# Eight slots for the first key pages of a paged attention step, and key pages fetched in four pieces of 32 keys

## The chip, the core and the metric

The kernel runs on one core of a Trainium2 chip. A core has five engines with a queue of instructions each: TensorE (PE in the profile; its weight loads stand as PEld), VectorE (DVE), ScalarE (ACT), GpSimd (POOL) and SyncE (SP). They wait for each other through semaphores. Data is moved between HBM and the on-chip memory (128 partitions) by 16 DMA engines; almost all of this kernel's transfers are issued from SP, in SP's program order. The metric is the time of one execution on the device, in microseconds (us).

## What is computed

One inference step of a decoder of two layers, in float32: a retention layer, then shared keys and values (K/V), then a block-sparse attention layer (MoBA). There are 256 prompt tokens and 8 sequences of 8 new tokens, the "sample", each with 256 past tokens. The past keys and values lie in a paged pool in HBM, and a table says which page belongs where:

```python
PAST_LEN, PAGE_SIZE, DEC_BATCH, DEC_SEQ = 256, 128, 8, 8
MOBA_HEADS, MOBA_HD = 8, 128
# cache_k, cache_v: (n_phys, PAGE_SIZE, MOBA_HEADS, MOBA_HD)    page_table: (8, 2)

def moba_sample(q, k_new, v_new, cache_k, cache_v, page_table, rel_bias):
    def per_seq(args):
        q_s, kn, vn, pages = args
        k_past = cache_k[pages].reshape(past, MOBA_HEADS, MOBA_HD)
        v_past = cache_v[pages].reshape(past, MOBA_HEADS, MOBA_HD)
        ...
        return moba_attend(q_s, q_pos, k_s, v_s, rel_bias)
```

So there are 16 key pages and 16 value pages, each of 128 tokens x 8 heads x 128 numbers, 512 KB. Every query scores all 256 past keys of its sequence and the new ones before it, per head; then softmax with a bias by distance, the sum over the values, a gate, and an output projection.

## The kernel before

All matrix products of the layers are done on one core. A projection's weights are cut into **chunks** of 1 MB: the list `chunks` holds them, and `make_schedule` writes one list of `steps` by hand. Each engine runs through the same list and does its own part of each step. So a step's place in the list is its place in every engine's queue. A chunk's weights land in one of three buffers of `w_raw` (`load_chunk`, issued two chunks ahead on SP, at the step `CHUNK`); ACT rounds them to `w_hi` (L1229) and DVE takes the rest, `w_lo` (L1569), a quarter at a time (steps `WS`); PE multiplies three terms of the two (L927, L930, L911). The chunks that matter here follow one another: four of the query projection (`mq`, up to about 330 us), four of the keys (`mk`, each 3 tiles in two halves), then four of the values (`mv`). The chunks `mk` and `mv` come from `w_kv`.

Among these the 16 **key pages** of the past are read and scored. A page n goes through these steps:

- On SP, `load_page` (L709): it waits until the slot is free, reads the page's number from `pages` into a register (L717), and issues the transfer. A key page is fetched in four pieces (L724). Piece g holds two heads of all 128 keys and goes to partitions 32g to 32g+31, four runs of 1 KB in each. A value page is one transfer to 128 partitions (L719). SP does these at the steps `ME` and `KP`.
- On DVE, the step `KP` n: a 32x32 block transpose of the page (L1860). It waits for `cache_loaded` of the slot and raises `kt_done`.
- On PE, the steps `KS` 0 to 3, each after four pages: 128 small matmuls (L1101) of the queries with the transposed keys.

Before the change there are six **slots** for key pages: four in `cache` and two in the tensor `mkT` (`early_pages`), which is free until the new keys are written to it. Page n takes slot n mod 6 for the first twelve pages, and one of the four in `cache` from then on. The first six pages are asked for without a wait, at `ME` 1 to 6. From page 6 on a page's load waits on `kt_done`: page 6 for the transpose of page 0, page 7 for that of page 1, and so on. SP's queue is in order, so whatever stands behind such a wait is issued after it, the weight chunks too. ACT waits with `KX`, its first write to `mkT`, until twelve pages are transposed (L1498), since the last pages that lie in `mkT` are 10 and 11.

The new value rows of the sample, `mvs`, and the new key rows, `rows`, are written later. POOL clears the unused half of `mvs` and of `rows` at the step `MB`, ahead of the queries' spread.

Of the kernel before, what the change touches and what calls it, by code (L numbers as in the profile page):

```python
# [33 lines left out]
P = 128  # L34
D = 1024
KT = D // P
TP, TS = 256, 64
# [3 lines left out]
MH, HD = 8, 128  # L41
# [7 lines left out]
NST = 8  # L49
NCP, NSLOT = 4, 6  # L50
FAR = PAST + NEW - 1
# [64 lines left out]


def page_slot(n):

    return n % NSLOT if n < 2 * NSLOT else (n - 2 * NSLOT) % NCP  # L120

# [190 lines left out]
def build(nc, a):  # L312
# [3 lines left out]
    with ctx:  # L316
# [3 lines left out]
        def sem(name):  # L320
            return ctx.enter_context(nc.semaphore(name))
# [90 lines left out]
        cache = mb("cache", [P, NCP, D])  # L412
# [3 lines left out]
        mvs = mb("mvs", [P, D])  # L416
        rows = mb("rows", [P, 3, 512])
# [75 lines left out]
        line_stored, lines_stored = sem("line_stored"), sem("lines_stored")  # L493
        bias_loaded, tb_loaded, bn_done = sem("bias_loaded"), sem("tb_loaded"), sem("bn_done")
        wide_cleared, pads_cleared = sem("wide_cleared"), sem("pads_cleared")
        wide_filled, wide_reset, kt_done, own_q_done = sem("wide_filled"), sem("wide_reset"), sem("kt_done"), sem("own_q_done")
# [67 lines left out]
        def page_at(n):  # L564

            at = page_slot(n)
            return cache[:, at, :] if at < NCP else early_pages[:, at - NCP, :]

# [98 lines left out]
        def _(sp):  # L667
# [41 lines left out]
            def load_page(n):  # L709

                m, vals = (n - 16, True) if n >= 16 else (key_page(n), False)
                before = n - (NCP if n >= 2 * NSLOT + NCP else NSLOT)
                if before >= 16:
# [4 lines left out]
                if vals:  # L718
                    sp.dma_start(page_at(n), a["cache_v"][bass.ds(page, 1)].rearrange("o p h d -> p (o h d)"))\  # L719
                        .then_inc(cache_loaded[page_slot(n)], 16)  # L720
                    return
                src = a["cache_k"][bass.ds(page, 1)].rearrange("o (c i) h d -> i (o c) (h d)", i=32)
                for g in range(4):
                    sp.dma_start(page_at(n)[32 * g:32 * g + 32, :].rearrange("p (c x) -> p c x", c=4), src[:, :, 256 * g:256 * g + 256])\  # L724
                        .then_inc(cache_loaded[page_slot(n)], 16)
# [19 lines left out]
            for step in steps:  # L745
# [65 lines left out]
                elif kind == "US":  # L811
                    store_pair(4 * step[1] + 3)
                    load_pair(4 * step[1] + 6)
                elif kind == "ME" and 1 <= step[1] <= NSLOT:
                    if step[1] == 1:
                        sp.wait_ge(pages_loaded, 16)
                        await_ret_over(sp)
                        sp.dma_start(knw[:, :], bass.AP(a["k_norm_w"].tensor, 0, [[0, P], [1, HD]])).then_inc(knw_loaded, 16)
                    load_page(step[1] - 1)
                elif kind == "KP":  # L820
                    n = step[1]
                    if 1 <= n <= 16 - NSLOT:
                        load_page(n + NSLOT - 1)
                    elif n >= 16 - NCP + 1:
                        load_page(n + NCP - 1)
                elif kind == "SE" and step[1] == 1:
# [30 lines left out]
        def _(pe):  # L857
# [83 lines left out]
            for step in steps:  # L941
# [221 lines left out]
                elif kind == "PN":  # L1163
                    pe.wait_ge(pads_cleared, 1)
                    await_read(pe, sb_bank(3), "SB", 3)
# [45 lines left out]
        def _(act):  # L1211
# [27 lines left out]
            for step in steps:  # L1239
# [257 lines left out]
                elif kind == "KX":  # L1497
                    act.wait_ge(kt_done, 2 * NSLOT)  # L1498
                    for i in range(2):
# [448 lines left out]
        def _(pool):  # L1948
# [28 lines left out]
            for step in steps:  # L1977
# [42 lines left out]
                elif kind == "MB":  # L2020
# [5 lines left out]
                    pool.wait_ge(wide_cleared, 1)  # L2026
                    pool.memset(mvs[TS:P, :], 0.0)
                    pool.memset(rows[TS:P, 2, :], 0.0)
# [5 lines left out]
                elif kind == "KS" and step[1] == 3:  # L2034
                    await_ks(pool, 3)
                    pool.wait_ge(bn_done, 1)
                    for n, g in enumerate((1, 3)):
                        if n:
                            pool.wait_ge(wide_reset, 1)
                        pool.memset(slots[32 * g:32 * g + 32, :, :, 16:16 + NEW], 0.0).then_inc(wide_reset, 1)  # L2040
# [53 lines left out]
```

## Time and profile before

| | us |
|---|---|
| median of 3 runs | 506.27 |
| lowest and highest of them | 503.84, 506.54 |
| the profiled execution, whole | 503.63 |
| its span in the trace | 501.6 |

| engine | busy us | share of the span |
|---|---|---|
| PE | 490.5 | 98% |
| PEld | 423.9 | 85% |
| DVE | 357.9 | 71% |
| ACT | 261.2 | 52% |
| POOL | 97.5 | 19% |

The profiled execution took 503.63 us, of which the trace's span holds 501.6; the 2.0 us between them lie around it. Times in the trace count from the span's start. PE is busy nearly all the time, so a wait matters where it stops PE; the profile's table of waits says which instruction was late and what ended its wait. The views of the DMA engines give three things for a stretch: the mean busy share of the 16 engines (a share over 1 means that packets overlap on an engine), the rate in GB/s, and how many packets were under 2 KB.

### The profile page before, as it was taken

The page shows a single profiled execution, that of the slowest core. Times are in us where ns is not written, and L with a number is a line of the kernel's source. Part 1 is how long each engine was busy: PE and PEld are TensorE (multiplying, and loading weights), DVE is VectorE, ACT ScalarE, POOL GpSimd, SP SyncE. Part 2 cuts the span into 40 slices and gives each one's busy share as a digit, 9 for nine tenths or more (in the row PEclk, how much of TensorE's full clock was granted, in tenths as well). Part 3 has the DMA queues.
Part 4 walks back from the last instruction along what each step waited for, and adds up shares of the span by engine and source line. Part 5 has one row for each costly group of instructions (what it writes and reads, how often), then busy time and mean ns, then how long its engine had stood idle before and what let it go on. Part 6 is the DMA issues. An engine that isn't in the chain of part 4 may idle for free.

```text
span 501.6 us, 9903 instructions
## 1 busy us (share of the span) xinstructions
PE 490.5 (98%) x3689; PEld 423.9 (85%) x3689; DVE 357.9 (71%) x633; ACT 261.2 (52%) x536; POOL 97.5 (19%) x139
## 2 busy tenths in 40 slices
PE   8999999999999999999999999999799999999997
PEld 6989978899778987799799999987567878999885
DVE  3955539884799819895589978996865764776662
ACT  6735532564427715366454455853637655655630
POOL 0291003620073200920000052454002000000000
PEclk9999999999999999999999999999999999999999
DMA  9993979999899898999936979979998567683211
GB/s 264 350 344 113 273 252 304 383 364 230 280 338 392 245 225 307 352 348 255 257 131 219 345 237 276 230 172 200 256 316 262 186 205 236 232 309 135 85 52 52
DMA packets 86771, 125.54 MB, mean 250 GB/s; under 512 B 5492, under 2 KB 51525, under 8 KB 86597
## 3 DMA queue, kind: packets, MB, share of 16 engines
q1 hardware_dynamic: 85874, 124.63, 80.7%
q8 instruction: 29, 0.48, 0.4%
q0 software_dynamic: 768, 0.28, 0.4%
q14 instruction: 18, 0.14, 0.1%
q10 hardware_dynamic: 82, 0.02, 0.0%
HBM read 98.93 MB, written 27.57 MB: 252 GB/s over the span
## 4 chain that ended last, share of the span: by engine, by line
PE 90%; DMA 3%; DVE 2%; ACT 2%; issue 2%; SPq 1%; POOL 0%; DVEq 0%; ACTq 0%; POOLq 0%
PE bank L930 46%; PE bank L927 17%; PE bank L911 7%; PE bank L1039 3%; DMA w_raw<-in_w_kv 2%; PE bank L1159 2%; PE bank L1053 1%; PE bank L986 1%; SPq L724 1%; PE bank L1205 1%; PE bank L1019 1%; PE bank L1021 1%; PE bank L1020 1%; PE bank L1007 1%; PE bank L1192 1%
## 5 line engine op out<-in xcount | busy, mean ns | idle before, releaser
L1569 DVE TENSOR_TENSOR w_lo<-w_raw,w_hi 128x512 fp32r<-128x512 f32 x207 | 143.2, 731 | 65.8 <-ACT w_hi L1229 65.0
L1229 ACT ACTIVATE w_hi<-w_raw 128x512 fp32r<-128x512 f32 x208 | 118.6, 620 | 71.6 <-PE bank L930 35.7
L930 PE MATMUL bank<-xn_hi,w_hi 128*128 128x320 f32 x320 | 100.2, 317 | 0.8 <-ACT w_hi L1229 0.7
L930 PE MATMUL bank<-xn_hi,w_lo 128*128 128x320 f32 x320 | 97.7, 309 | 0.1
L930 PE MATMUL bank<-xn_lo,w_hi 128*128 128x320 f32 x320 | 97.6, 309 | 0.0
L927 PE MATMUL bank<-w_hi,xn_hi 128*128 128x512 f32 x160 | 64.8, 405 | 0.0
L930 PEld LDWEIGHTS bank<-xn_hi,w_hi 128*128 128x128 f32 x320 | 59.7, 188 | 5.0 <-issue 2.9
L927 PE MATMUL bank<-w_lo,xn_hi 128*128 128x512 f32 x160 | 62.5, 391 | 0.0
L927 PE MATMUL bank<-w_hi,xn_lo 128*128 128x512 f32 x160 | 62.5, 390 | 0.0
L930 PE MATMUL bank<-ym_hi,w_hi 128*128 128x320 f32 x192 | 60.9, 317 | 0.0
L930 PEld LDWEIGHTS bank<-xn_lo,w_hi 128*128 128x128 f32 x320 | 59.8, 188 | 0.4 <-DVE xn_lo L1618 0.2
L930 PEld LDWEIGHTS bank<-xn_hi,w_lo 128*128 128x128 f32 x320 | 59.7, 188 | 0.3 <-DVE w_lo L1569 0.3
L930 PE MATMUL bank<-ym_hi,w_lo 128*128 128x320 f32 x192 | 59.3, 309 | 0.0
L930 PE MATMUL bank<-ym_lo,w_hi 128*128 128x320 f32 x192 | 59.3, 309 | 0.0
L1788 DVE SCALAR_TENSOR_TENSOR st<-st,bank 128x512 f32<-128x512 f32 x64 | 39.7, 684 | 5.2 <-PE bank L1053 5.2
L1997 POOL TENSOR_TENSOR fin<-raw_qk,cst 128x320 f32<-128x320 f32 x16 | 17.3, 1101 | 109.3 <-DMA out_ret_state_prompt<-fin 101.7
L930 PEld LDWEIGHTS bank<-ym_hi,w_hi 128*128 128x128 f32 x192 | 36.1, 188 | 1.8 <-issue 1.7
L927 PEld LDWEIGHTS bank<-w_hi,xn_hi 128*128 128x128 f32 x160 | 30.0, 188 | 8.6 <-issue 3.1
L930 PEld LDWEIGHTS bank<-ym_lo,w_hi 128*128 128x128 f32 x192 | 36.1, 188 | 0.1
L930 PEld LDWEIGHTS bank<-ym_hi,w_lo 128*128 128x128 f32 x192 | 36.0, 188 | 0.0
L927 PEld LDWEIGHTS bank<-w_lo,xn_hi 128*128 128x128 f32 x160 | 30.1, 188 | 6.6
L927 PEld LDWEIGHTS bank<-w_hi,xn_lo 128*128 128x128 f32 x160 | 30.1, 188 | 5.5
(289 smaller groups left out, 783.6 us busy)
## 6 DMA issues: line engine op xcount, KB each, us to landing
w_raw<-in_ret_w_in SPq DMA_DIRECT2D x23, 1024.0 KB, 11.3
st<-in_state_ret SPq DMA_DIRECT2D x32, 512.0 KB, 8.6
out_ret_state_sample<-st SPq DMA_DIRECT2D x32, 512.0 KB, 4.5
w_raw<-in_ret_w_out SPq DMA_DIRECT2D x8, 1024.0 KB, 8.5
w_raw<-in_moba_w_in SPq DMA_DIRECT2D x8, 1024.0 KB, 6.5
w_raw<-in_w_kv SPq DMA_DIRECT2D x8, 1024.0 KB, 8.7
cache<-in_cache_v SPq DMA_DIRECT2D x16, 512.0 KB, 4.8
cache<-in_cache_k SPq DMA_DIRECT2D x48, 128.0 KB, 5.7
```

The lines of the kernel that those rows point to most:

```text
L724: sp.dma_start(page_at(n)[32 * g:32 * g + 32, :].rearrange("p (c x) -> p c x", c=4), src[:, :, 256 * g:256 * g + 256])\
L911: mm = pe.matmul(bank[b][:, :], xn_hi[:, k, TP:T + TS], w[:, wk, :], start=k == 0 and n == 0, stop=k == KT - 1 and n == 1)
L927: mm = pe.matmul(bank[b][0:m, :], x[:, k, c0:c0 + m], w[:, wk, :], **flags)
L930: mm = pe.matmul(bank[out][:, 0:T], w[:, wk, P * tile:P * tile + P], x[:, k, :], **flags)
L986: mm = pe.matmul(bank[5][0:m, col:col + n], kT[:, d, j:j + m], qT[:, d, i0:i0 + n], start=d == 0, stop=d == 1)
L1007: mm = pe.matmul(o[:, P:TP], vp[:, 1, at], sT_own[:, :], start=False, stop=True)
L1039: mm = pe.matmul(bank[5][32 * j:32 * j + 32, :], qz[:, q0:q0 + 32], st[:, b, DV * d:DV * d + DV], start=False, stop=g == 1 and d == 1, ski ...
L1159: mm = pe.matmul(bank[7][32 * j:32 * j + 32, P * u:P * u + P], window(8 * half_at + 4 * (j // 2) + 2 * pg + j % 2, b % 4), page_at(16 + m) ...
L1229: act.activation(w_hi[:, c % 2, part], w_raw[:, c % RAW, part], ACT.Copy).then_inc(w_hi_done, 1)
L1569: dve.tensor_tensor(w_lo[:, c % 2, part], w_raw[:, c % RAW, part], w_hi[:, c % 2, part].bitcast(F32), ALU.subtract).then_inc(w_lo_done, 1)
L1788: dve.scalar_tensor_tensor(state, state, math.exp(NEW * LOG_DECAY[h]), bank[up_bank(b, d)][:, :], ALU.mult, ALU.add).then_inc(bank_read[up ...
L1997: done(pool.tensor_tensor(to, x, tab, ALU.mult))
```

## The change

The number of slots goes from six to eight. Pages 0 to 7 each have one of their own: four in `cache`, two in `mkT`, one in `mvs` and one in the first two thirds of `rows`. All eight are asked for without a wait, at `ME` 1 to 6. Pages 8 to 15 take the slots 0, 1, 2, 3, 6, 1, 2, 3 again, and a table (`ORDERED_AT`) says at which step `KP` each of pages 8 to 18 is asked for. Each of these waits for the transpose of the page that held its slot before. ACT's wait at `KX` is for six pages instead of twelve, since only pages 4 and 5 lie in `mkT`. POOL's clearing of half of `mvs` moves behind the last transpose, to the step `KS` 3, and PE's `PN` waits for it.

The four pieces of a key page are cut in another way. Piece c now holds 32 keys with all 8 heads: it goes to all 128 partitions, one run of 1 KB in each. On the HBM side its outermost dimension is the four pairs of heads, inside it the 32 keys. Where every byte of the page lies on the chip in the end is the same as before.

```diff
-NCP, NSLOT = 4, 6
+NCP, NSLOT = 4, 8
...
+LATE_SLOTS = (0, 1, 2, 3, 6, 1, 2, 3)
+ORDERED_AT = {8: 1, 9: 2, 10: 3, 11: 4, 12: 7, 13: 10, 14: 11, 15: 12, 16: 13, 17: 14, 18: 15}
...
 def page_slot(n):
-    return n % NSLOT if n < 2 * NSLOT else (n - 2 * NSLOT) % NCP
+    return n if n < NSLOT else LATE_SLOTS[n - NSLOT] if n < 16 else (n - 16) % NCP
+
+def slot_before(n):
+    return max((m for m in range(n) if page_slot(m) == page_slot(n)), default=-1)
...
         def page_at(n):
             at = page_slot(n)
-            return cache[:, at, :] if at < NCP else early_pages[:, at - NCP, :]
+            if at < NCP:
+                return cache[:, at, :]
+            return (early_pages[:, 0, :], early_pages[:, 1, :], mvs[:, :], rows[:, 0:2, :].rearrange("p t x -> p (t x)"))[at - NCP]
...
                 m, vals = (n - 16, True) if n >= 16 else (key_page(n), False)
-                before = n - (NCP if n >= 2 * NSLOT + NCP else NSLOT)
+                before = slot_before(n)
...
-                src = a["cache_k"][bass.ds(page, 1)].rearrange("o (c i) h d -> i (o c) (h d)", i=32)
-                for g in range(4):
-                    sp.dma_start(page_at(n)[32 * g:32 * g + 32, :].rearrange("p (c x) -> p c x", c=4), src[:, :, 256 * g:256 * g + 256])\
+                src = a["cache_k"][bass.ds(page, 1)].rearrange("o (c i) h d -> (o c) i (h d)", i=32)
+                for c in range(4):
+                    sp.dma_start(page_at(n)[:, 256 * c:256 * c + 256], src[c].rearrange("i (g x) -> g i x", g=4))\
                         .then_inc(cache_loaded[page_slot(n)], 16)
...
-                elif kind == "ME" and 1 <= step[1] <= NSLOT:
+                elif kind == "ME" and 1 <= step[1] < MH - 1:
...
-                    load_page(step[1] - 1)
+                    for n in ((), (0, 1), (2,), (3,), (4,), (5, 6), (7,))[step[1]]:
+                        load_page(n)
                 elif kind == "KP":
-                    n = step[1]
-                    if 1 <= n <= 16 - NSLOT:
-                        load_page(n + NSLOT - 1)
-                    elif n >= 16 - NCP + 1:
-                        load_page(n + NCP - 1)
+                    for n, at in ORDERED_AT.items():
+                        if at == step[1]:
+                            load_page(n)
...
                 elif kind == "PN":
-                    pe.wait_ge(pads_cleared, 1)
+                    pe.wait_ge(mvs_cleared, 1)
...
                 elif kind == "KX":
-                    act.wait_ge(kt_done, 2 * NSLOT)
+                    act.wait_ge(kt_done, 6)
...
-                    pool.memset(mvs[TS:P, :], 0.0)
                     pool.memset(rows[TS:P, 2, :], 0.0)
...
+                    pool.memset(mvs[TS:P, :], 0.0).then_inc(mvs_cleared, 1)
+                    pool.wait_ge(mvs_cleared, 1)
```

How the instructions stand: SP's queue before the change, from the end of page 5's load over page 6's to the weight chunk behind it (`w_raw` is the chunk's buffer, `mkT` and `cache` are the page's slots, the size is that of one piece on the chip's side).

```order
L724 DMA mkT<-in_cache_k 32x4x256
L717 TENSOR_LOAD pages [waits kt_done]
L717 ISA x2
L724 ISA
L724 DMA cache<-in_cache_k 32x4x256
...
L724 DMA cache<-in_cache_k 32x4x256
L682 DMA w_raw<-in_w_kv 128x4x512 [waits w_lo_done]
L717 TENSOR_LOAD pages [waits kt_done]
```

The same place of SP's queue after the change, from the end of page 6's load over pages 7 and 8 to the same weight chunk.

```order
L736 DMA mvs<-in_cache_k 128x1x256
L729 TENSOR_LOAD pages
L729 ISA x2
L736 ISA
L736 DMA rows<-in_cache_k 128x1x256
...
L729 TENSOR_LOAD pages [waits kt_done]
...
L736 DMA cache<-in_cache_k 128x1x256
L694 DMA w_raw<-in_w_kv 128x4x512 [waits w_lo_done]
L729 TENSOR_LOAD pages [waits kt_done]
```

Page 8 is now the first whose load waits for a transpose, where it was page 6. In front of this weight chunk (the third of the keys) stand nine pages instead of seven, and in front of the fourth thirteen, as before. The first value chunk, that had all sixteen in front of it, now has fifteen. Every piece has gone from 32 partitions of four runs to 128 partitions of one.

DVE's queue before the change, at the transposes of pages 6 to 8, with the split of weights between them:

```order
L1860 STREAM_TRANSPOSE mvp<-cache 128x1024 [waits bank_full5,cache_loaded0,dve_steps]
L1860 STREAM_TRANSPOSE mvp<-cache 128x1024 [waits bank_full5,cache_loaded1]
L1569 TENSOR_TENSOR w_lo<-w_raw,w_hi 128x512 [waits w_hi_done] x2
L1860 STREAM_TRANSPOSE ktc<-cache 128x1024 [waits ks_done,cache_loaded2]
L1595 TENSOR_TENSOR rows<-bank,rows 64x512 [waits half_done,knw_loaded]
```

and after it:

```order
L1871 STREAM_TRANSPOSE mvp<-mvs 128x1024 [waits bank_full5,cache_loaded6,dve_steps]
L1871 STREAM_TRANSPOSE mvp<-rows 128x1024 [waits bank_full5,cache_loaded7]
L1580 TENSOR_TENSOR w_lo<-w_raw,w_hi 128x512 [waits w_hi_done] x2
L1871 STREAM_TRANSPOSE ktc<-cache 128x1024 [waits ks_done,cache_loaded0]
L1606 TENSOR_TENSOR rows<-bank,rows 64x512 [waits half_done,knw_loaded]
```

Nothing moves on DVE; only the slot read and its semaphore differ. PE's and ACT's queues have the same instructions in the same order too.

## Rows read from the trace of the kernel before

**Rows 1.** The page: the span, and busy time by engine.

```profile
span 501.6 us, 9903 instructions
...
PE 490.5 (98%) x3689; PEld 423.9 (85%) x3689; DVE 357.9 (71%) x633; ACT 261.2 (52%) x536; POOL 97.5 (19%) x139
```

**Rows 2.** Three stretches; columns: length, busy us (x instructions) by engine, PEclk, DMA share, GB/s.

```profile
300.00:350.00 50.00, 50.00 (x541) 44.20 (x541) 41.84 (x68) 27.82 (x66) 21.50 (x52) 1.00 0.97 216
350.00:385.00 35.00, 29.93 (x365) 21.64 (x364) 25.74 (x43) 19.56 (x51) 3.71 (x9) 1.00 0.98 275
385.00:502.00 117.00, 113.11 (x920) 97.47 (x917) 70.47 (x164) 59.79 (x147) 0.00 (x0) 1.00 0.49 169
```

**Rows 3.** Waits between 300 and 420 us: total us, times, longest.

```profile
ACT w_hi L1229 <- DMA w_raw<-in_w_kv: 6.4, 2, 4.8
...
PE bank L911 <- DVE w_lo L1569: 1.9, 1, 1.9
...
PE bank L1116 <- ACT mkT L1501: 1.4, 1, 1.4
```

**Rows 4.** SP's issues between 300 and 385 us: start, length, what.

```profile
301.71 4.47 SPq L724 DMA_DIRECT2D cache<-in_cache_k  x8
306.63 0.40 SPq L682 DMA_DIRECT2D w_raw<-in_w_kv  x1
...
328.61 1.82 SPq L724 DMA_DIRECT2D cache<-in_cache_k  x4
...
349.15 0.40 SPq L682 DMA_DIRECT2D w_raw<-in_w_kv  x1
...
358.74 0.40 SPq L682 DMA_DIRECT2D w_raw<-in_w_kv  x1
```

**Rows 5.** The chain of waits, 340 to 385 us: start, length, what.

```profile
349.15 11.57 DMA w_raw<-in_w_kv
```

**Rows 6.** DMA in short stretches; columns: length, PE, PEclk, DMA share, GB/s.

```profile
46.00:48.00 2.00, 2.00 (x16) 1.00 0.53 189
302.00:303.50 1.50, 1.50 (x13) 1.00 1.09 388
...
304.00:305.00 1.00, 1.00 (x9) 1.00 1.16 283
305.00:308.00 3.00, 3.00 (x22) 1.00 1.15 210
310.00:311.50 1.50, 1.50 (x12) 1.00 1.05 371
```

**Rows 7.** Packets of one of these, 305 to 308 us.

```profile
DMA packets 693, 0.63 MB, mean 210 GB/s; under 512 B 78, under 2 KB 693, under 8 KB 693
```

**Rows 8.** DMA issues by tensor: count, KB each, median us to landing.

```profile
w_raw<-in_w_kv SPq DMA_DIRECT2D x8, 1024.0 KB, 8.7
cache<-in_cache_v SPq DMA_DIRECT2D x16, 512.0 KB, 4.8
...
v_rows<-vs_split SPq DMA_DIRECT2D x16, 128.0 KB
```

**Rows 9.** SP, issue of narrow and wide transfers: ns min/median/max.

```profile
L772 SPq DMA_DIRECT2D v_rows<-vs_split x4: 570/584/692, 44.0 to 46.0; - x4
L786 SPq DMA_DIRECT2D vq<-v_rows x4: 432/432/461, 50.0 to 51.4; - x4
```

**Rows 10.** Transposes of the pages on DVE: ns min/median/max, first and last start.

```profile
L1860 DVE STREAM_TRANSPOSE mvp<-cache x4: 1234/1240/1245, 339.0 to 367.2; 128x1024 f32<-128x1024 f32 x4
```

**Rows 11.** The last scoring step's start on PE.

```profile
373.95 0.44 PE L1101 MATMUL bank<-tb,wide 32*32 32x256 f32 x8
```

**Rows 12.** POOL: the clearing of mvs, and the stretch after the last scores.

```profile
300.02 0.95 POOL L2027 MEMSET mvs<- 64x1024 f32 x1
...
379.64 0.89 POOL L2045 COPY scr<-mqT 128x256 f32<-128x256 f32 x2
```

**Rows 13.** The product that takes POOL's result, on PE.

```profile
388.40 1.10 PE L1136 MATMUL bank<-mkT,scr 128*32 128x64 f32 x64
```

More of the change, by code:

```diff
@@ L494, in build @@
         bias_loaded, tb_loaded, bn_done = sem("bias_loaded"), sem("tb_loaded"), sem("bn_done")
+        mvs_cleared = sem("mvs_cleared")
         wide_cleared, pads_cleared = sem("wide_cleared"), sem("pads_cleared")
```

## The prediction

> **What bounds the kernel now.** I read the page first: PE is busy for 490.5 of 501.6 us [rows 1], so only the stretches in which PE idles can give anything back. The table of stretches finds them: from 350 to 385 us PE is busy for 29.93 of 35 us, so 5.07 us are idle; from 300 to 350 us it never idles [rows 2]. The waits name two stops of PE: 1.9 us for a `w_lo` and 1.4 us for an `mkT` copy [rows 3]. Behind both is ACT, which waited 6.4 us for weights of `w_kv` [rows 3]. SP's queue shows why these came late: one such chunk was issued at 349.15, with seven pages ahead of it in the queue whose loads wait for transposes [rows 4], and took 11.57 us to land [rows 5], where 8.7 is the median [rows 8]. So the key pages cost the kernel at most 5.07 us. Last I read the DMA engines' rate, since that is what the change touches with every page. A chunk of 1 KB runs moves at 388 GB/s; with key pages alone the same engines are full (share 1.15) and move 210 [rows 6], and every packet there is under 2 KB as well [rows 7]. The difference to the first is the destination: 32 partitions in each piece, not 128.
>
> **Part 1: the new pieces.** Both ways move 128 runs of 1 KB per piece, 64 pieces in all. What differs is how a transfer is shared among the 16 DMA engines. The trace has one kind of transfer whose two sides differ in shape as the new pieces' do: `v_rows` is written with an outermost dimension of 8 from a tile of 64 partitions. While four of these are in flight, the DMA share is 0.53 at 189 GB/s [rows 6], which is half of the engines: 189 GB/s over 0.53 x 16 engines is 22 GB/s for each busy one, and 388 over 1.09 x 16 is 22 as well. The same transfers have no time to landing in the list of issues, where the wide ones have one [rows 8]. So I read: the number of engines is set by the outermost dimension, and by the smaller side of the two. The new pieces have 128 on the chip's side and 4 on the HBM side. I take it that each runs on 4 engines, and that all 64 use the same four.
>
> The Trainium skill says this in one rule (DMA: Bandwidth & Descriptors, section "Why a DMA increments its semaphore by 16 and not by 1"): the engines used are the largest number up to 16 that divides the slowest dimension of both sides, and they are the lowest-numbered ones. The 0.53 share of `v_rows` agrees with it; no row of before has 4 on the HBM side.
>
> Price of a page on 4 engines: each moves 128 KB, 131,072 bytes. At 388/16 = 24.3 GB/s that is 5.40 us; at the 22.2 GB/s by busy share, 5.90. Both rest on the same row [rows 6], so I take the middle, 5.65 us, and keep the ends for the range. Before, a page took 524,288 bytes at 210 GB/s, 2.50 us. A weight chunk still uses all 16 engines, 64 KB on each: 65,536 at 24.3 GB/s is 2.70 us on each of the four too, and it lands only when they have done their share. SP's transfers stand in order on an engine, as I assume here, so pages and chunks queue on the four.
>
> Does SP keep them fed? A narrow transfer took SP 584 ns to issue, a wide one 432 [rows 9]; a page before took 1.82 us [rows 4] plus about 0.45 for its number. Four pieces at 584 with the registers' work make at most 3.5 us, under 5.65. So SP runs ahead, the eight first pages wait for nothing, and the later loads wait for transposes of pages four to eight places ahead of them, done long before the engines come to them.
>
> The sum along the four engines: the chunk in flight ends at about 304.0 (283 GB/s in the us after it, 210 from 305 on [rows 6]). Then 16 pages, 16 x 5.65 = 90.4, and the five `w_kv` chunks that stand in front of page 15, 5 x 2.70 = 13.5. The last byte of page 15 lands at 304.0 + 103.9 = 407.9. DVE turns it in 1.24 [rows 10], and half a microsecond goes to the semaphores (my estimate): 409.6. The last scoring step, `KS` 3, cannot start before; it started at 373.95 [rows 11]. Shift: **35.7 us**. It contains the whole of the idle time that PE has now, and PE would wait at the start of each key chunk and at each `KS` instead, some 40 us in all.
>
> Behind `KS` 3 two things are late in addition. DVE's queue has the reductions of three tiles and four splits between page 15's transpose and the first value chunk: 6 to 8 us of work against some 6 us of PE's; I take 1 us, bounds 0 to 3. And PE runs at the higher of its two levels, 2.4 GHz (granted clock 1.00), in all rows of this stage [rows 2], where it never idled for long. After waits of several us it may be granted 1.2 GHz, which would double the 3 us of `KS` 3: 1 us, bounds 0 to 3. Together 35.7 + 2 = **37.7 us**.
>
> **Part 2: eight slots and the order.** Two more pages in front of the first wait, page 8 waits where page 6 did. By itself this would take SP's waits from in front of the weights and could give back part of the 5.07 us. With pages at 5.65 us the engines, not SP, set every arrival, so I book nothing. If the pages were wide, this part would count; it stands in the first rival.
>
> **Part 3: the small moves.** The transposes read `mvs` and `rows` in the form in which they read `cache`, 1.24 us each: 0. POOL's clearing of `mvs`, 0.95 us, goes behind the last scores; POOL is then done at about 380.5 + 1 [rows 12], while PE takes the result at 388.40 [rows 13]: hidden with 6 us to spare, 0; if that cover were gone it would cost 0.95. ACT's wait at `KX` falls from twelve pages to six. It did not hold ACT (its wait was for weights [rows 3]): 0, and a gain is excluded since what it waits for next is a tile behind the pages' chain.
>
> **The sum.** 503.63 + 37.7 = 541.3 us. The profiled execution is 2.6 us under the median of 506.27, and inside the three runs' spread of 503.84 to 506.54 but for 0.2 us.
>
> **The rivals.**
>
> *A. The pieces use all 16 engines (faster, or no change).* Decides: whether the smaller outermost dimension on the source side narrows a transfer as one on the destination side does. Against it: the `v_rows` rows. For it: no row has this very shape. A page would then move at 388 GB/s, 1.35 us instead of 2.50, so 16 pages take 18 us less of engines that are full now, the chunks issued at 349.15 and 358.74 [rows 4] would land some 6 to 9 us earlier, and the two stops of PE would go: 503.6 - 3.3 = **500.3 us**, between 498.5 (all 5.07) and 504 (nothing). The Trainium skill has the rule behind this case (SBUF — State Buffer, section "Door 1: The DMA port swizzle"): partitions 0 to 31 reach half of the ports of 0 to 127. The 210 against 388 GB/s agree with it. By it alone the change is a gain; what it leaves out is the count of engines.
>
> *B. Four engines that also get in each other's way (slower still).* Engine 0 would write partitions 0 to 31 and engine 1 partitions 32 to 63, in step, and so on. Today's pieces show what two engines cost each other on the same partitions' way in: 210 GB/s over 1.15 x 16 engines, 11.4 GB/s for each. A page would take 131,072 / 11.4 = 11.5 us: 304.0 + 184 + 13.5 + 1.7 = 503.2, shift 129, **634 us**. Clashing half of the time, 8.5 us a page, gives 304.0 + 136 + 13.5 + 1.7 = 455.2, shift 81, and with the 2 us of above 587. For it: the packets of today's pages. Against it: eight engines reading 64 partitions for `v_rows` kept 22 GB/s each.
>
> *C. Narrow, but the weights pass the pages.* If chunks did not queue behind pages, the chain is 304.0 + 90.4 + 1.7 = 396.1, shift 22: **528 us** with the 2 us. Against it: all are SP's and go out in order.
>
> **How the numbers follow.** My forecast (4 engines, 535 to 549) has 0.60, A 0.12, B 0.18, C 0.10. The predicted time is the likeliest case's, 541. Its own range: 5.40 us a page gives 4 less, 5.90 gives 4 more, the late ends 2 less to 4 more, so 535 to 549. For 8 in 10 I go down to C, 525, and up to the half-clashing B, 590; A (0.12) and the worse half of B (0.08) are left out. A measurement of this kernel tells about 0.5% from no change. Faster by more: 0.08, the better part of A; the same: 0.04; slower: 0.88.
>
> **What would show it.** In the trace of after: a DMA share near 0.25 to 0.4 at about 90 to 100 GB/s wherever only pages are in flight (A: 1.1 at 380; B: 0.25 at 50); key pages without a time to landing; the transpose of page 15 at about 408 instead of 367 [rows 10]; waits of DVE's transposes for `in_cache_k` of tens of us in total, where the last page's is now hidden; 35 to 45 us of idle PE between 330 and 412; weights of `w_kv` landing 15 to 30 us after issue. I am wrong if the share in those stretches is near 1, or if the chunks land in 6 us between late pages.

## The result and the profile after

| | kernel before | changed kernel |
|---|---|---|
| median, us | 505.28 (503.84 to 506.54, 4 runs) | **555.86** (555.14 to 556.61, 4 runs) |
| ratio, 95% interval | 1 | **1.0996** [1.0955, 1.1038] |
| profiled execution: whole / span, us | 503.63 / 501.6 | 555.9 / 553.9 |
| PE idle between 300 and 421 us | 5.1 | 38.2 |
| last scoring step (`KS` 3) starts on PE, us | 373.95 | 421.49 |

The changed kernel is 50.6 us slower. 541.3 was forecast, with a range of 525 to 590. The line numbers of the engines' steps are 10 to 12 higher than before: L724 is L736, and L1101 is L1112. Each ratio here and below is to the kernel before as it ran on the same occasion; its median there was between 505.28 and 506.62 us.

First the page of the changed kernel: busy time, then the granted clock, the DMA share and GB/s in 40 slices, and the chain of waits by line.

```profile
span 553.9 us, 9903 instructions
...
PE 506.6 (91%) x3689; PEld 433.7 (78%) x3689; DVE 358.8 (65%) x633; ACT 260.7 (47%) x536; POOL 97.2 (18%) x139
...
PEclk9999999999999999999999997886677899999999
DMA  9984969998999999994697245342458737667211
GB/s 270 352 300 123 334 236 357 364 256 270 346 365 221 261 339 388 250 253 154 222 348 231 90 143 141 104 144 89 143 153 295 269 109 261 212 232 256 89 47 47
...
PE bank L941 36%; PE bank L938 15%; SPq L736 12%; PE bank L922 5%; PE bank L1050 3%; SPq L729 2%; DMA w_raw<-in_w_kv 2%; PE bank L1170 1%; PE bank L1064 1%; PE bank L997 1%; SPq L694 1%; DMA st<-in_x_prompt 1%; PE bank L1216 1%; DVE w_lo L1580 1%; PE bank L1030 1%
```

The span grows by 52.3 us and PE's busy time by 16.1, though PE has the same 3,689 instructions as before [rows 1]. So most of the loss is idle time, and the rest is work done at a lower granted clock: slices 24 to 31 fall to between 6 and 8 tenths. The DMA line falls to between 2 and 5 in slices 22 to 29, and 12% of the chain is now SP's issuing of key pages.

The stretches of the changed kernel (columns as in [rows 2]):

```profile
300.00:350.00 50.00, 40.38 (x256) 36.26 (x255) 33.50 (x58) 24.15 (x57) 13.80 (x40) 0.90 0.44 132
350.00:385.00 35.00, 19.04 (x303) 13.26 (x301) 13.34 (x19) 8.20 (x21) 7.83 (x17) 0.84 0.39 117
385.00:421.00 36.00, 23.37 (x186) 16.87 (x186) 11.61 (x17) 6.33 (x15) 0.00 (x0) 0.68 0.55 173
...
375.00:380.00 5.00, 2.21 (x5) 1.82 (x6) 4.15 (x7) 3.31 (x8) 0.00 (x0) 0.50 0.27 89
```

In the two stretches of [rows 2], PE was idle for 0 and 5.07 us; now it is idle for 9.6 and 16.0, and for 12.6 more up to 421. The last row is a stretch with key pages alone: a share of 0.27 at 89 GB/s, where the old pieces had 1.15 at 210 [rows 6]. The granted clock there is 0.50, the lower of PE's two levels (1.2 GHz).

Who waits, between 300 and 440 us (total us, times, longest):

```profile
ACT w_hi L1240 <- DMA w_raw<-in_w_kv: 51.8, 5, 21.0
...
DVE mvp L1871 <- DMA cache<-in_cache_k: 12.0, 2, 7.2
...
PE bank L1085 <- ACT mvp L1302: 9.1, 1, 9.1
...
PE bank L922 <- DVE w_lo L1580: 8.9, 3, 4.7
...
DVE scr L1871 <- DMA cache<-in_cache_k: 6.4, 2, 4.1
...
DVE mvp L1871 <- DMA rows<-in_cache_k: 5.0, 1, 5.0
```

ACT's wait for weights was 6.4 us [rows 3] and is 51.8. These weights are not slow to land, they are issued late. The longest wait, 21.0 us, ends with the chunk that SP issued at 361.23, which had landed 10.6 us later; the chunk in its place in the queue before, the third of the keys, was issued at 330.53. DVE's transposes wait 23.4 us for key pages in these three rows, against 3 us before. SP's queue shows how the pages go out now (start, length, what):

```profile
301.90 14.90 SPq L736 DMA_DIRECT2D cache<-in_cache_k  x12
316.91 1.20 SPq L694 DMA_DIRECT2D w_raw<-in_w_kv  x1
...
363.50 18.63 SPq L736 DMA_DIRECT2D cache<-in_cache_k  x12
...
405.66 5.60 SPq L736 DMA_DIRECT2D cache<-in_cache_k  x4
```

Three pages took 18.63 us of SP, 6.2 for each, where one took 1.82 [rows 4]. That is close to the 5.89 us that a page takes four engines at 89 GB/s (524,288 bytes), so I read it that SP waits inside its issue instructions until the queue has room. The key pages have no time to landing in the list of issues:

```profile
w_raw<-in_w_kv SPq DMA_DIRECT2D x8, 1024.0 KB, 10.6
cache<-in_cache_v SPq DMA_DIRECT2D x16, 512.0 KB
cache<-in_cache_k SPq DMA_DIRECT2D x44, 128.0 KB
```

But neither have the value pages, whose one wide transfer is as it was before (4.8 us in [rows 8]). So the missing time is no sure mark of a narrow transfer.

The last page is turned by DVE, and PE starts behind it:

```profile
420.19 1.25 DVE L1871 STREAM_TRANSPOSE mvp<-cache 128x1024 f32<-128x1024 f32 x1 [7.16 <-DMA cache<-in_cache_k]
...
421.49 0.57 PE L1112 MATMUL bank<-tb,wide 32*32 32x256 f32 x8 [2.52 <-DVE mvp L1871]
```

`KS` 3 is 47.5 us later than in [rows 11]. From there to the end of the span it takes 132.4 us, against 127.7 before, which is the remaining 4.8.

### The profile page after: what moved, and what is told of

It reads as the page before. It is cut to its first block, busy times and chain, and to the rows that moved or that the text cites. A ratio compares the mean times of both kernels' runs of the same rounds, so it can differ in the third digit from the quotient of the medians.

```text
span 553.9 us, 9903 instructions
## 1 busy us (share of the span) xinstructions
PE 506.6 (91%) x3689; PEld 433.7 (78%) x3689; DVE 358.8 (65%) x633; ACT 260.7 (47%) x536; POOL 97.2 (18%) x139
## 4 chain that ended last, share of the span: by engine, by line
PE 73%; SPq 16%; issue 4%; DMA 3%; DVE 2%; ACT 1%; DVEq 0%; ACTq 0%
PE bank L941 36%; PE bank L938 15%; SPq L736 12%; PE bank L922 5%; PE bank L1050 3%; SPq L729 2%; DMA w_raw<-in_w_kv 2%; PE bank L1170 1%; PE bank L1064 1%; PE bank L997 1%; SPq L694 1%; DMA st<-in_x_prompt 1%; PE bank L1216 1%; DVE w_lo L1580 1%; PE bank L1030 1%
## 5 line engine op out<-in xcount | busy, mean ns | idle before, releaser
L1580 DVE TENSOR_TENSOR w_lo<-w_raw,w_hi 128x512 fp32r<-128x512 f32 x207 | 143.3, 730 | 92.2 <-ACT w_hi L1240 91.5
L1240 ACT ACTIVATE w_hi<-w_raw 128x512 fp32r<-128x512 f32 x208 | 118.6, 620 | 110.4 <-DMA w_raw<-in_w_kv 51.8
L938 PE MATMUL bank<-w_hi,xn_hi 128*128 128x512 f32 x160 | 68.6, 428 | 0.2 <-DVE w_lo L1580 0.2
L938 PE MATMUL bank<-w_hi,xn_lo 128*128 128x512 f32 x160 | 65.8, 411 | 0.0
L938 PE MATMUL bank<-w_lo,xn_hi 128*128 128x512 f32 x160 | 65.6, 410 | 0.0
L922 PE MATMUL bank<-w_hi,xn_hi 128*128 128x512 f32 x80 | 34.7, 433 | 16.3 <-DVE w_lo L1580 8.9
L938 PEld LDWEIGHTS bank<-w_hi,xn_hi 128*128 128x128 f32 x160 | 32.2, 201 | 10.1 <-issue 3.4
L938 PEld LDWEIGHTS bank<-w_lo,xn_hi 128*128 128x128 f32 x160 | 32.1, 201 | 7.4
L2008 POOL TENSOR_TENSOR fin<-raw_qk,cst 128x320 f32<-128x320 f32 x16 | 18.1, 1150 | 109.7 <-DMA out_ret_state_prompt<-fin 102.1
L938 PEld LDWEIGHTS bank<-w_hi,xn_lo 128*128 128x128 f32 x160 | 32.3, 202 | 6.2
## 6 DMA issues: line engine op xcount, KB each, us to landing
w_raw<-in_w_kv SPq DMA_DIRECT2D x8, 1024.0 KB, 10.6
```

The costliest lines, as they stand in the source:

```text
L922: mm = pe.matmul(bank[b][:, :], xn_hi[:, k, TP:T + TS], w[:, wk, :], start=k == 0 and n == 0, stop=k == KT - 1 and n == 1)
L938: mm = pe.matmul(bank[b][0:m, :], x[:, k, c0:c0 + m], w[:, wk, :], **flags)
L1240: act.activation(w_hi[:, c % 2, part], w_raw[:, c % RAW, part], ACT.Copy).then_inc(w_hi_done, 1)
L1580: dve.tensor_tensor(w_lo[:, c % 2, part], w_raw[:, c % RAW, part], w_hi[:, c % 2, part].bitcast(F32), ALU.subtract).then_inc(w_lo_done, 1)
L2008: done(pool.tensor_tensor(to, x, tab, ALU.mult))
```

## The experiments

All experiments change only how key pages are fetched, or what stands beside them. The theory: the number of DMA engines of a transfer follows the outermost dimension of its HBM side, the new pieces have 4 there, and pages and weights queue on the same four engines.

### 1. The two halves of the change

Slots and order alone: the changed kernel with these lines for L734 to L737.

```diff
-src = a["cache_k"][bass.ds(page, 1)].rearrange("o (c i) h d -> (o c) i (h d)", i=32)
-for c in range(4):
-    sp.dma_start(page_at(n)[:, 256 * c:256 * c + 256], src[c].rearrange("i (g x) -> g i x", g=4))
+src = a["cache_k"][bass.ds(page, 1)].rearrange("o (c i) h d -> i (o c) (h d)", i=32)
+for g in range(4):
+    sp.dma_start(page_at(n)[32 * g:32 * g + 32, :].rearrange("p (c x) -> p c x", c=4), src[:, :, 256 * g:256 * g + 256])
```

> The changed kernel with the old pieces: each page in four pieces of 32 partitions with four runs of 1 KB per partition. So the eight slots, the new order of pages, the moved clearing and the shorter wait of ACT stand alone. Theory (the loss is all in the pieces): pages take 2.5 us again as before, KS 3 starts near 374 and not at 421.49, and the kernel is where it was, 498 to 506 us, with any gain no more than the 5 us that PE idled between 350 and 385 us before. Rival (the slots or the new order cost something too, for instance because the first weights of w_kv now stand behind eight pages): 508 to 520 us, with PE idle before 350.

Measured: 502.34 us, ratio 0.9939 [0.9905, 0.9973]. `KS` 3 starts at 372.91, and PE's idle time from 350 to 385 us is 2.4 us, half of what it was:

```profile
350.00:385.00 35.00, 32.58 (x426) 24.23 (x403) 26.91 (x44) 20.59 (x53) 4.51 (x10) 1.00 0.93 279
```

The pieces alone: the kernel before with the three `-` lines in place of the `+` lines.

> The kernel before with only the new pieces: six slots and the old order of pages stay. Theory (the pieces are all of the loss): about 4 us more or less than the changed kernel, 548 to 562 us, with DMA share near 0.27 at 89 GB/s while pages alone are in flight. If a part of the 50 us is due to the slots or to the order, this stays under 540 us. If the eight slots saved something behind narrow pieces, it is over 562.

Measured: 556.57 us, ratio 1.0996 [1.0938, 1.1054], with `KS` 3 at 419.87. The new pieces are the whole loss. The slots are worth 3 us with the old pieces and nothing measurable with the new ones.

The old pieces in another order:

```diff
-for g in range(4):
+for g in (0, 2, 1, 3):
```

> As the run above, but the four old pieces of a page are issued for partition groups 0, 2, 1, 3 and not 0, 1, 2, 3. If the 210 GB/s of old pages come from neighbouring pieces in flight that write partitions of one half of the chip's memory side, the share-to-rate relation changes (over 250 GB/s with pages alone) and the stretch from 300 to 350 us gains 1 to 3 us of waits. If each piece of 32 partitions is slow by itself, whatever is beside it, the rate stays at 200 to 220 GB/s and the time is that of the run above within 0.3%.

Measured: 501.45 us, ratio 0.9902 [0.9866, 0.9937]. This is the fastest of the kernels that compute the reference's outputs. Whether the order adds anything to the slots is open, since the two intervals overlap. The rates of full engines do not settle it either. From 308 to 310 us, pages alone, they are higher than with the slots alone (this run first, then the slots alone), from 340 to 345 they are the same (1.16 and 209 there):

```profile
308.00:310.00 2.00, 2.00 (x15) 2.00 (x15) 1.97 (x2) 0.00 (x0) 0.00 (x0) 1.00 1.14 231
```

```profile
308.00:310.00 2.00, 2.00 (x16) 2.00 (x15) 2.00 (x2) 0.00 (x0) 0.00 (x0) 1.00 1.15 210
```

```profile
340.00:345.00 5.00, 5.00 (x101) 3.76 (x78) 3.66 (x6) 1.16 (x2) 4.93 (x9) 1.00 1.17 210
```

So neither answer named beforehand holds throughout: 231 is above the 200 to 220 GB/s of the one and below the 250 of the other.

### 2. The outermost dimension: 2, 4, 8, 16

The same pieces to the same 128 partitions in runs of 1 KB, with `A` = 16 or 8:

```diff
-src[c].rearrange("i (g x) -> g i x", g=4)
+src[c].rearrange("i (g x) -> (i g) x", g=4).rearrange("(b a) x -> a b x", a=A)
```

> The changed kernel with one thing different in the pieces: the 128 runs of a piece are read from the same 128 KB in another order, so that the outermost dimension on the HBM side is 16 and not 4. Pieces, bytes, runs of 1 KB, the 128 partitions written and the number of transfers stay. The keys then land on other partitions, so the attention computed is not the reference's; the amount of work is the same. Theory (the number of DMA engines follows the outermost dimension of the HBM side): all 16 engines, share over 1.0 and over 350 GB/s with pages alone, a page in under 1.5 us, KS 3 near 372, and 497 to 505 us. Rival 1 (a piece over 128 partitions from runs of 1 KB is slow by itself, or SP's four issues per page set the pace): 89 GB/s and 550 to 560 us as in the changed kernel. Rival 2 (it is the order in which keys are read from HBM): something between, 89 to 210 GB/s and 510 to 545 us.

> The same with 8 as outermost dimension (keys on other partitions, attention not the reference's). Theory: 8 engines, share near 0.54 at 178 GB/s when pages alone keep them fed, a page of 524,288 bytes in 2.94 us. The engines' sum is 304 + 16 x 2.94 + 5 x 3.6 = 369 us, 5 us before the last scoring step needs page 15, and SP's own issuing (2.7 us and more for four pieces, as seen with 16) then sets the pace: 502 to 509 us, like the run with 16. Rival (only 16 gives more than four engines; anything else falls back to few): near 556 us.

> Control for the run with 16 as outermost dimension, which took 503.8 us: the same scrambled reading order (a key of 4 KB in four neighbouring pieces of 1 KB), the same pieces, bytes and partitions, but the outermost dimension on the HBM side is 4 again. The keys land on other partitions, so the attention is not the reference's. Theory (the outermost dimension sets the number of engines): 4 engines, share near 0.27 at 89 GB/s, 550 to 561 us like the changed kernel. Rival (the reading order within HBM was what helped): near 504 us.

The last is no control after all: with `A` = 4 the two rearrangements give exactly the addresses of the changed kernel. It is a repeat of it on another occasion.

> The changed kernel with each new piece cut into two of 64 partitions, outermost dimension 2 on the HBM side, 8 pieces for a page. All of the computation stays. Theory (engines by the outermost dimension, always the same lowest ones): 2 engines at 22.3 GB/s each, share near 0.14 at 45 GB/s, a page in 11.8 us, the last scoring step 16 x 5.9 = 94 us later than in the changed kernel, so 640 to 665 us. Rival 1 (each transfer picks engines of its own, so that two halves share the work): 550 to 565 us. Rival 2 (SP's issuing sets the pace, by transfer): twice the transfers at 0.6 us, at most 32 x 0.6 = 19 us more than now, 556 to 580 us.

```diff
-sp.dma_start(page_at(n)[:, 256 * c:256 * c + 256], src[c].rearrange("i (g x) -> g i x", g=4))
+for half in range(2):
+    sp.dma_start(page_at(n)[64 * half:64 * half + 64, 256 * c:256 * c + 256],
+                 src[c].rearrange("i (g x) -> g i x", g=4)[2 * half:2 * half + 2])
```

| outermost dimension | us | ratio [95%] | `KS` 3 starts |
|---|---|---|---|
| 2 (8 pieces a page) | 648.23 | 1.2798 [1.2681, 1.2914] | 512.96 |
| 4 (changed kernel) | 555.86 | 1.0996 [1.0955, 1.1038] | 421.49 |
| 4 again | 556.73 | 1.1013 [1.0929, 1.1097] | 422.23 |
| 8 | 516.37 | 1.0198 [1.0124, 1.0272] | 382.68 |
| 16 | 503.79 | 0.9939 [0.9909, 0.9969] | 372.06 |

Stretches with pages alone, of the run with 2, then 8, then 16 (last two columns: DMA share, GB/s):

```profile
345.00:350.00 5.00, 3.54 (x9) 2.82 (x10) 5.00 (x8) 3.33 (x9) 1.87 (x8) 0.55 0.14 45
```

```profile
306.00:308.00 2.00, 2.00 (x16) 2.00 (x15) 2.00 (x4) 0.51 (x1) 0.00 (x0) 1.00 0.54 178
308.00:310.00 2.00, 2.00 (x15) 2.00 (x15) 1.97 (x2) 0.00 (x0) 0.00 (x0) 1.00 0.40 119
```

```profile
306.00:308.00 2.00, 2.00 (x16) 2.00 (x15) 2.00 (x4) 0.90 (x2) 0.00 (x0) 1.00 0.80 245
308.00:310.00 2.00, 2.00 (x16) 2.00 (x15) 2.00 (x2) 0.00 (x0) 0.00 (x0) 1.00 0.51 153
```

With 2, 4 and 8 the highest shares are 0.14, 0.27 and 0.54 at 45, 89 and 178 GB/s: each step doubles both, and it is 22.3 GB/s for each engine used. That is the theory. With 16 the pages do not always fill the engines, but where a few are queued the share is 0.80 at 245 GB/s, and in the first half of that stretch (306 to 307) 1.00 at 292. Eight engines at 22.3 GB/s would move 178, so more than eight are at work. The order in which the 128 runs are read from HBM changes too with 8 and 16, and the run meant as its control was none. The account does not need one: the rate per engine is the same for 2, 4 and 8, and only their number grows. Two engines delay `KS` 3 by 91.5 us against four; 94 was expected. The rule of the Trainium skill (DMA: Bandwidth & Descriptors, section "Why a DMA increments its semaphore by 16 and not by 1") gives these numbers of engines, and the runs agree with it for the source side: exactly for 2, 4 and 8, and for 16 as far as more than eight.

But 8 cost 7.4 us more than the upper end expected. Its second row shows why: the share is 0.40, under the 0.54 that eight full engines show, so the engines wait for work. SP's queue in that run (start, length, what), and one of its issue instructions against those of the run with 16, of the changed kernel and of the old pieces (ns min/median/max):

```profile
331.35 3.11 SPq L736 DMA_DIRECT2D mvs<-in_cache_k  x4
335.76 3.11 SPq L736 DMA_DIRECT2D rows<-in_cache_k  x4
340.19 3.11 SPq L736 DMA_DIRECT2D cache<-in_cache_k  x4
...
L736 SPq DMA_DIRECT2D cache<-in_cache_k x44: 604/622/1317, 302.7 to 375.5; - x44
```

```profile
L736 SPq DMA_DIRECT2D cache<-in_cache_k x44: 538/539/1207, 303.4 to 364.5; - x44
```

```profile
L736 SPq DMA_DIRECT2D cache<-in_cache_k x44: 537/1153/2113, 301.9 to 410.2; - x44
```

```profile
L724 SPq DMA_DIRECT2D cache<-in_cache_k x48: 316/318/1445, 301.7 to 358.3; - x48
```

With 8, a page takes SP 4.43 us (335.76 to 340.19): four issues and 1.3 us for the page's number. Its eight engines need 2.94. With 16 an issue is 539 ns, against 318 for the old pieces. With 4 the shortest is about the same and the median 1,153: there SP is held by the full queue.

### 3. Is it SP that limits the wider pieces?

The page number is read once, and one page is fetched 16 times, which takes some 1.2 us of SP's work from each with 8, and 0.8 with 16 (a page's issues end at 333.12 there and the next page's begin at 333.90).

```diff
-page = sp.value_load(pages[0:1, m:m + 1], ...)
+if vals or n == 0:
+    key_row[0] = page = sp.value_load(pages[0:1, m:m + 1], ...)
+page = page if vals else key_row[0]
```

> The run with outermost dimension 8 (516.4 us; keys on other partitions), in which SP reads the page number once and fetches the same page of keys 16 times, so the attention is not the reference's and the bytes moved are the same. This takes about 1.2 us of SP's work from each page. Theory (with 8 engines it is SP that sets the pace, 4 x 0.62 us of issuing and 1.3 us of the number's load and registers in 4.4 us a page, while a page takes the engines 2.94 us): SP's last page is issued 10 to 15 us earlier, and the time falls to 502 to 508 us. Rival (8 engines are too few in themselves, or the distance from issue to landing is what counts): 514 to 518 us.

Measured: 510.72 us (508.48 to 513.70 over its ten runs), against 516.37. `KS` 3 starts at 378.08, not at 382.68. SP was a limit, but only 5.7 us go and not 8 to 14; the time lies between the theory's range and the rival's. The stretches say what is next:

```profile
325.00:330.00 5.00, 5.00 (x36) 5.00 (x35) 5.00 (x8) 3.98 (x10) 1.82 (x9) 1.00 0.54 180
330.00:335.00 5.00, 5.00 (x30) 3.84 (x32) 4.83 (x7) 2.58 (x6) 1.75 (x7) 1.00 0.54 173
```

The share is 0.54, eight full engines, so now they are the limit. Both theories held a part. That it is always the same page has not made it quicker on the engines: 0.54 at 180 GB/s is what the run with 8 showed (178).

> The run with outermost dimension 16 (503.8 us; keys on other partitions), with the page number read once and the same page of keys fetched 16 times, so the attention is not the reference's and the bytes are the same. It takes about 1.2 us of SP's work from each page. Theory (with pieces over 16 engines SP's issuing, 0.54 us a piece against 0.32 for the old pieces, was what kept the wide page from giving its whole gain): SP's last key page is issued before 358 us instead of 362.3, the stop of PE at 385.9 for rows goes, and the time is 498 to 501.5 us. Rival (something else behind KS 3 costs the 3 us): 502.5 to 505 us as before.

Measured: 500.00 us, ratio 0.9873 [0.9833, 0.9913], 3.8 us under the run with 16 that reads each number. Of the two traces compared here, this one is of a middling run (499.90), but that of the other is the slowest of its ten (506.66, where the median is 503.79), so the traces show more of a difference than the medians. The last key page is issued at 356.89 (362.32 there):

```profile
356.89 2.47 SPq L739 DMA_DIRECT2D cache<-in_cache_k  x4
```

PE is busy for 33.81 of the 35 us from 350 to 385, and its stop of 2.15 us behind `KS` 3 is gone:

```profile
350.00:385.00 35.00, 33.81 (x421) 25.33 (x405) 26.60 (x43) 21.41 (x54) 3.69 (x6) 1.00 0.79 260
```

### 4. Do the weights queue on the four engines?

```diff
+if c in first_kv:                      # the first five w_kv chunks
+    to, src = to[:, 0:KT // 4], src[:, 0:KT // 4]
 sp.dma_start(to, src).then_inc(w_loaded[c % RAW], 16)
```

> The changed kernel, with only the first half (512 KB of 1 MB) loaded of each of the five w_kv chunks that stand between the pages; the other half of the tile keeps old weights, so keys and values are not the reference's. Multiplications and waits stay. Theory (the chunks' share queues on the same four engines as the pages, 3.56 us for each whole chunk as the dips in the trace of the changed kernel show): KS 3 starts 5 x 1.8 = 9 us earlier, near 412.5, and the time is 545 to 550 us against 555.9. Rival (chunks go beside the pages on the twelve other engines and their share on the four costs nothing): no change, 553 to 558 us.

Measured: 546.86 us (ratio 1.0819 [1.0753, 1.0885]), 9.0 less than the changed kernel. `KS` 3 starts 7.7 us earlier:

```profile
413.75 0.45 PE L1115 MATMUL bank<-tb,wide 32*32 32x256 f32 x8 [1.01 <-DVE mvp L1874]
```

So a whole chunk costs the chain 2 x 7.74 / 5 = 3.1 us (7.74 is 421.49 less 413.75). The case in which weights pass the pages is out.

### 5. Half of the pages narrow

The new pieces for pages 0 to 7 (`if n < 8:`), the old ones for 8 to 15.

> The changed kernel with new pieces for the first eight pages and the old pieces for the last eight. Theory (one queue on four engines, then SP's pace): the first eight pages take 8 x 5.9 us plus two chunks, and SP issues the ninth near 355 as in the changed kernel (330.4 with old pieces only). Eight old pages at 2.6 us of SP, three chunks and one wait then take 25 to 31 us as with old pieces only: last page issued at 380 to 386 and not at 411, KS 3 near 386 to 392, and 515 to 523 us. So about two thirds of the loss would come with the last eight pages, because the slack of SP and of the engines covers a part of the first eight. Rival (loss in proportion to the number of narrow pages): half of the 50 us, 528 to 532 us.

Measured: 533.73 us, ratio 1.0548 [1.0479, 1.0618]: 28 of the 50 us. That is nearest to the rival's proportion (528 to 532) and not the third that the theory gave. `KS` 3 starts at 405.04. SP issued the ninth page at 356.61, as expected. But then it was held:

```profile
375.53 0.40 SPq L694 DMA_DIRECT2D w_raw<-in_w_kv  x1
383.80 4.50 SPq L742 DMA_DIRECT2D cache<-in_cache_k  x8
...
389.56 1.82 SPq L742 DMA_DIRECT2D cache<-in_cache_k  x4
```

From 375.93 to 383.80 SP waits for a slot whose page has not been turned (the table of waits has 7.1 us for a transpose into `ktc`), since DVE and PE are late themselves. What the theory had counted as slack in the second half is a wait for the first half, and it moves with it. With old pieces alone the same wait stands between 345.1 and 352.3 (6.5 us in the table).

### 6. What ends last at page 15

The changed kernel, with one wait on SP ahead of the first value page:

```diff
+if n == 16:
+    sp.wait_ge(kt_done, 16)
```

> The changed kernel with one wait more on SP: the first value page, and with it everything issued behind it (a second value page, the stores of keys and one w_kv chunk), goes out only when page 15 of the keys has been transposed. All of the computation stays. In the changed kernel the first value page was issued at 412.56 and two pages' worth of wide transfers moved at 241 to 395 GB/s between 415 and 420 us, while page 15 was still on its way. Theory (transfers issued later share the four engines with page 15, they do not stand behind it in order): page 15 lands 2 to 4 us earlier, KS 3 starts at 417.5 to 419.5 and not at 421.49. The total is then 553 to 559 us, because the w_kv chunk behind is issued later too. Rival (transfers stand in order on an engine, and page 15 itself took until 420): KS 3 starts at 421 to 422 all the same.

Measured: 561.42 us, above the range expected, since all that stands behind the wait on SP is later. `KS` 3 starts at the same time, so the theory falls:

```profile
421.46 0.68 PE L1114 MATMUL bank<-tb,wide 32*32 32x256 f32 x8 [2.82 <-DVE mvp L1873]
```

The wide transfers moving beside page 15 cost it nothing. With them gone the end of the four engines' queue can be seen:

```profile
416.00:418.00 2.00, 2.00 (x6) 1.56 (x6) 0.00 (x0) 0.00 (x0) 0.00 (x0) 0.57 0.27 89
...
418.00:418.50 0.50, 0.50 (x3) 0.19 (x1) 0.00 (x0) 0.00 (x0) 0.00 (x0) 1.00 0.17 55
418.50:419.00 0.50, 0.14 (x1) 0.00 (x0) 0.00 (x0) 0.00 (x0) 0.00 (x0) 1.00 0.14 45
419.00:419.50 0.50, 0.00 (x0) 0.00 (x0) 0.00 (x0) 0.00 (x0) 0.00 (x0) 1.00 0.07 25
...
420.16 1.25 DVE L1873 STREAM_TRANSPOSE mvp<-cache 128x1024 f32<-128x1024 f32 x1 [6.65 <-DMA cache<-in_cache_k]
```

The shares 0.27, 0.17, 0.14 and 0.07 read as engines that end one after another between 418 and 419.5, in the mean at about 418.7 (62,500 bytes move after 418, which is 0.7 us at 89 GB/s). A page has landed only with the last of them, and the transpose follows 0.6 us later.

## Why the prediction was right, and where it was off

**The mechanism was right.** Pieces whose HBM side has 4 outermost use four engines. Most marks that were named are in the trace: a share of 0.27 at 89 GB/s, key pages without a time to landing (a weak mark, as said), 23 us of DVE's waits, and 35.1 us of idle PE between 330 and 412. The transpose of page 15 came at 420.19, 12 us behind the 408 named. One mark was missed: the chunks of `w_kv` were to land 15 to 30 us after issue, and the five in question landed 10.6 to 11.3 us after it. What the runs showed in its place is that SP, which was to run ahead of the engines, was held by the full queue and issued the weights late. The four engines were kept fed all the same (share 0.27 wherever pages were alone), and so the sum did not suffer. The series from 2 to 16 is the proof of the number of engines. Rivals A, B and C are out: A by 0.27 against 1.1, B by the 22.3 GB/s that each of the four kept, C by the halved chunks.

**The sum was 14.6 us short**, 541.3 against 555.9 in the profiled execution. Its terms one by one:

- *A page: 5.65 booked, 5.89 measured* (524,288 bytes at 89 GB/s). It was the upper end. The rate by busy share was right, and the rate by 16 whole engines too high. 16 pages: +3.8 us.
- *A chunk: 2.70 booked, 3.1 measured* by the halved chunks. Five: +2.0.
- *Other traffic on the four engines: 0 booked.* From 304.2 to 418.7, the mean end in the run with the later value pages, are 114.5 us; pages and chunks make 94.2 + 15.5 = 109.7. The other 4.8 went to what else moved there, by subtraction. The stretches from 350 to 358 us, with a share of 0.40 to 0.42, hold POOL's 16 loads of `bs`. Which transfer took how much was not measured apart.
- *From the mean end to the transpose: 0.5 booked, 1.5 measured* (418.7 to 420.16): four engines do not end together, and the step to the semaphore comes on top. +1.0. With 0.2 us of start this makes the shift 47.5 instead of 35.7.
- *Behind `KS` 3: 2 us booked, 4.8 measured.* It is more the queues of DVE and ACT than the clock. Three runs with late pages have a granted clock of 1.00 from `KS` 3 to the end, and there this stretch takes 131 us: 130.8 with 8 engines (513.5 - 382.68), 131.0 with 8 engines and one number, 130.9 with the halved chunks. That is 3.3 over the 127.7 of before. The other 1.5 in the changed kernel go with its clock, 0.66 in the 5 us from the start of `KS` 3 and 0.89 to 0.94 in the 20 behind them. PE stops there for rows that ACT turns late, in the changed kernel and, with a `w_lo` as well, in the trace of the run with 16, where the clock fell to 0.87 behind the stops and the stretch took 132.5 us:

```profile
435.21 1.46 PE L1127 MATMUL bank<-eye,rows 128*128 128x128 f32 x6 [2.13 <-ACT rows L1505]
```

```profile
381.44 0.50 PE L939 MATMUL bank<-w_hi,xn_hi 128*128 128x512 f32 x1 [1.60 <-DVE w_lo L1581]
385.92 1.29 PE L1128 MATMUL bank<-eye,rows 128*128 128x128 f32 x6 [2.15 <-ACT rows L1506]
```

In the run with one number and 16 engines that part is 126.8 us again (498.0 - 371.18). My bounds of 0 to 3 for the queues and 0 to 3 for the clock held the total; the 3.3 of the queues is a little over its own.

**SP's pace was mis-seen.** A narrow issue was taken at 584 ns and a page at 3.5 us of SP. The run with 8 shows 4.43 for pieces of this kind. That was under the 5.89 of the engines and so cost nothing here. But rival A was priced without it: 500.3 us forecast, 503.79 measured with 16 engines, and 500.00 once SP had less to do. So the price of A was right only for an SP that is not in the way. Its term for a page was too low as well: A has 388 GB/s for wide pages, and full engines moved them at 292 (share 1.13 from 317 to 319 us in the run with one number), which makes 1.8 us a page and not 1.35.

**Parts 2 and 3 at 0** were right for the new pieces: with and without them the new pieces take 556 us. That eight slots help once pages are wide was said under rival A, and is measured with the old pieces: 3 us.

## What to carry to other kernels

Before rearranging a DMA's source, look at the outermost dimension of both sides: 2, 4 or 8 there meant 2, 4 or 8 engines, however many partitions the destination has. In the profile the mark is a DMA share that stands at a quotient of 16 (0.14, 0.27, 0.54) while an engine waits for data. Such a transfer is paid by everything behind it in the queue, so price it by the sum along the engines it uses, and add the other traffic on them; before calling a later wait slack, ask whether it is a wait for the late thing itself. And price the issues: a transfer that is quicker on the engines can cost the issuing engine more.

## What the runs showed that I had not expected

- SP's issue of 128 KB in 128 runs of 1 KB took 318 ns for 32 partitions with four runs each, 539 ns over 128 partitions with 16 outermost on the HBM side, and 622 ns with 8 (medians; the same bytes and number of runs). Why the shape costs this is open.
- Issue instructions behind a narrow transfer stretch: 1,153 ns in the median and 2,113 at most in the changed kernel, from 537 at least. The queue's pressure is seen in SP's own instruction, not as a wait.
- The four engines seem to end their queue up to 1.5 us apart (the share falls in steps from 418.0 to 419.5).
- The old pieces filled all 16 engines (share 1.16) at 209 GB/s; wide pieces on full engines moved 292 at 1.13, 1.4 times as much. Yet without SP's relief the time was the same as with the old ones and eight slots (503.79 and 502.34, both with ratio 0.9939).
